# Products on unnormalised chunks ahead of three norms of a two-block fp32 kernel

## What is computed

```python
def modulate(x, g, shift, scale):
    return rms_norm(x, g) * (1 + scale[:, None, :]) + shift[:, None, :]
def swiglu(h, w1, w3, w2):
    return (jax.nn.silu(h @ w1) * (h @ w3)) @ w2
...
        h = modulate(x, norm_g[l, 0], mod[:, 0, 0], mod[:, 0, 1])
        x = x + 0.5 * mod[:, 0, 2][:, None, :] * swiglu(h, ffn1_w1[l], ffn1_w3[l], ffn1_w2[l])
        h = modulate(x, norm_g[l, 1], mod[:, 1, 0], mod[:, 1, 1])
        y = hybrid_mixer(h, w_in[l], fox_f_bias[l], fox_qk_g[l], dsa_qk_g[l], w_br_fox[l], w_br_dsa[l], w_out[l], rope_a, rope_i, top_k)
        x = x + mod[:, 1, 2][:, None, :] * y
        h = modulate(x, norm_g[l, 2], mod[:, 2, 0], mod[:, 2, 1])
        x = x + 0.5 * mod[:, 2, 2][:, None, :] * swiglu(h, ffn2_w1[l], ffn2_w3[l], ffn2_w2[l])
```

## Time and profile before

| | us |
|---|---|
| median of 3 runs | 1995.74 |
| lowest and highest | 1994.92, 1996.67 |
| span of the profiled execution, first to last instruction | 1992.7 |
| TensorE busy (matmuls) | 1961.6 |
| VectorE, ScalarE, GpSimd busy | 901.8, 747.8, 825.9 |
| useful products end and start again around norm 3 | 838.8, 848.3 |
| around norm 4 | 1215.5, 1223.9 |
| around norm 5 | 1616.1, 1624.2 |

### The profile page before, as it was taken

The page is one execution under the profiler, slowest core; times in us unless marked ns, Lnnn a source line. Parts: engine busy times, 40 slices in busy tenths (PEclk is TensorE's granted clock), DMA queues, the critical chain, the costliest instruction groups (busy, mean ns, idle before and its releaser), DMA issues.

```text
span 1992.7 us, 25487 instructions
## 1 busy us (share of the span) xinstructions
PE 1961.6 (98%) x9250; PEld 1552.8 (78%) x9250; DVE 901.8 (45%) x1457; ACT 747.8 (38%) x1241; POOL 825.9 (41%) x361
## 2 busy tenths in 40 slices
PE   7999999999999999999999999999999999999998
PEld 6877656688888888888888888776767878888887
DVE  6772565432632453457662204777872242101111
ACT  5343555432431232333313324436673243222321
POOL 4365321243554345435543443333444434443442
PEclk9999999999999999999999999999999999999999
DMA  6355111243656477548643343332123333333341
GB/s 180 88 142 134 32 44 43 55 102 102 169 155 192 122 186 201 138 118 212 172 105 95 84 116 71 78 75 53 33 54 76 94 75 94 101 100 95 86 115 53
DMA packets 154565, 211.14 MB, mean 106 GB/s; under 512 B 15432, under 2 KB 129640, under 8 KB 154344
## 3 DMA queue, kind: packets, MB, share of 16 engines
q1 hardware_dynamic: 140232, 167.34, 34.0%
q10 hardware_dynamic: 14240, 42.54, 7.1%
HBM read 206.69 MB, written 2.10 MB: 105 GB/s over the span
## 4 chain that ended last, share of the span: by engine, by line
PE 49%; issue 33%; POOL 14%; DVE 2%; DMA 1%; ACT 1%; POOLq 0%; ACTq 0%; SPq 0%; DVEq 0%
PE ps L670 15%; PE ps L672 15%; PE ps L671 15%; POOL wlo L620 13%; PE ps L1164 1%; PE ps L1188 1%; PE ps L769 1%; DMA xrow<-in_x 0%; DVE score L2384 0%; PE ps L787 0%; PE ps L1208 0%; DVE xT L2415 0%; PE ps L950 0%; PE ps L718 0%; DVE st L2006 0%
## 5 line engine op out<-in xcount | busy, mean ns | idle before, releaser
L620 POOL TENSOR_TENSOR wlo<-raw,whi 128x1024 fp32r<-128x1024 f32 (+1 forms) x317 | 779.8, 2475 | 1037.3 <-ACT whi L1458 1015.6
L670 PE MATMUL ps<-hhi,whi 128*128 128x512 f32 x1496 | 592.9, 396 | 7.6 <-POOL wlo L620 3.5
L672 PE MATMUL ps<-hhi,wlo 128*128 128x512 f32 x1496 | 584.2, 390 | 0.0
L671 PE MATMUL ps<-hlo,whi 128*128 128x512 f32 x1496 | 583.7, 390 | 0.0
L1458 ACT ACTIVATE whi<-raw 128x1024 fp32r<-128x1024 f32 x309 | 316.7, 1055 | 385.4 <-PE ps L672 359.6
L670 PEld LDWEIGHTS ps<-hhi,whi 128*128 128x128 f32 x1496 | 281.4, 188 | 75.5 <-issue 12.6
L672 PEld LDWEIGHTS ps<-hhi,wlo 128*128 128x128 f32 x1496 | 281.2, 188 | 59.5
L671 PEld LDWEIGHTS ps<-hlo,whi 128*128 128x128 f32 x1496 | 281.6, 188 | 56.7 <-issue 1.2
L670 PE MATMUL ps<-hidhi,whi 128*128 (+1 forms) x608 | 236.8, 390 | 0.0
L672 PE MATMUL ps<-hidhi,wlo 128*128 (+1 forms) x608 | 236.8, 389 | 0.0
L671 PE MATMUL ps<-hidlo,whi 128*128 (+1 forms) x608 | 236.8, 389 | 0.0
(11 more groups left out here) (401 smaller groups left out, 2353.5 us busy)
## 6 DMA issues: line engine op xcount, KB each, us to landing
raw<-in_ffn_w SPq DMA_DIRECT2D x264, 256.0 KB, 3.8
raw<-in_w_in SPq DMA_DIRECT2D x154, 256.0 KB, 4.0
trig<-in_ada_w ACTq DMA_DIRECT2D x72, 512.0 KB, 4.7
raw<-in_w_up SPq DMA_DIRECT2D x64, 256.0 KB, 4.0
raw<-in_w_down SPq DMA_DIRECT2D x64, 256.0 KB, 3.9
raw<-in_w_out SPq DMA_DIRECT2D x32, 256.0 KB, 3.7
xrow<-in_x ACTq DMA_DIRECT2D x4, 512.0 KB, 6.2
raw<-in_cmp_k_w SPq DMA_DIRECT2D x8, 256.0 KB, 3.7
```

The costliest lines, as they stand in the source:

```text
L620: last = pool.tensor_tensor(lo, src, hi.bitcast(F32), ALU.subtract)
L670: pe.matmul(out_, lhi, rhi, start=first, stop=False)
L671: pe.matmul(out_, lhi, rlo, start=False, stop=False)
L672: return pe.matmul(out_, llo, rhi, start=False, stop=last)
```

## The change

At each of the norms 3, 4 and 5 the first four slabs behind it (96 products) use gain times x, split in XHI (ScalarE) and XLO (VectorE) as soon as a chunk of xT is there, in place of h. The filler is gone. The parts:

- GpSimd makes the five adds of squares (`squares`), between the halves of slabs; VectorE makes XLO in that place. TensorE sums total and last two squares by token (12 matmuls of one column, each two rows of the trace, as before) ahead of the third slab, and spreads half a slab later. ScalarE copies the spread row from PSUM to rstd in SBUF, and VectorE's norm reads it there.
- The banks of these first products are scaled afterwards by VectorE (TENSOR_TENSOR ps, rstd) and the shift's share is added as a bias: sigmoid with bias on ScalarE for the gates, (st + bias) * tmp on VectorE.
- The bias is shift times weights. In the down stage ahead, ScalarE issues four transfers of 512 KB of the first columns of the weights into the place of hhi (`shift_weights`), VectorE adds up 16 weighted pieces of 128x256 (`weight_shifts`), TensorE sums them over the partitions in two pairs (`shift_sums`), and VectorE copies each pair to bias (`biases`).
- In norm 4 the queries (blocks 0 and 1 of fox) are such products.

```diff
@@ pe projection
+                            unscaled = name == "fox" and n < 2
+                            opening = 2 if name == "fox" else 0
...
+                                if unscaled and n == 1:
+                                    square_sums(4) if q == 0 else shift_sums(4, 0)
...
+                                    if unscaled and n == 1 and q == 0 and x == 4:
+                                        norm(4)
...
+                            if unscaled and n == 1:
+                                shift_sums(4, 1)
+                                pe.wait_ge(bias_ready, 2 * STAT[4])
@@ pe ffn_up
+                if h == 0:
+                    blocks(0, True, {2: lambda: square_sums(nn), 3: lambda: shift_sums(nn, 0)})
+                    if f == 0:
+                        turn_modulation(4)
+                    shift_sums(nn, 1)
@@ gpsimd
+            def squares(n):
+                e = STAT[n]
+                for m in range(1, KD - 2):
+                    pool.wait_ge(n_sq, 8 * (e - 1) + m + 1)
+                    if m > 1:
+                        pool.wait_ge(n_add, 5 * (e - 1) + m - 1)
+                    pool.tensor_tensor(SQUARES[m], SQUARES[m - 1], SQUARES[m], ALU.add).then_inc(n_add, 1)
+                if n == 3:
+                    low(AT[FIRST[n]] + 1)
...
-            lows(AT["mixb1"] + SLOTS, AT["mixa2"] + SLOTS)
+            lows(AT["mixb1"] + SLOTS, AT["f1up0"] + 1)
+            squares(3)
+            lows(AT["f1up0"] + 2, AT["fox"] + 2)
+            squares(4)
@@ scalar norm
                         sc.wait_ge(x_ready, X_BEFORE_NORM[n] + m + 1)
+                        sc.activation(XHI[n][m], xT[:, m, :], ACT.Identity, scale=GAIN[n][:, m:m + 1]).then_inc(x_hi, 1)
...
+                    if n != 4:
+                        sc.activation(early[:, n + 2:n + 3], col(C_EPS), ACT.Sigmoid)
+                    high(s0 + SLOTS)
+                    sc.wait_ge(n_all, e + 1)
+                    sc.activation(rstd[:, :], ps[:, 7, :], ACT.Copy).then_inc(rows_ready, 1)
@@ scalar, first_chunks of a ffn_up
+                    high(s0 + 2)
+                    for c in range(2):
+                        sc.wait_ge(ff_m2, u0 + c + 1)
+                        sc.activation(hidhi[:, c, :], tmp[:, 2 + c, :], ACT.Copy).then_inc(ff_hi, 1)
+                    high(s0 + 3)
@@ vector
+            def biases(n, pair):
+                x = 2 * (STAT[n] - 1) + pair + 1
+                ve.wait_ge(ws_sum, x)
+                ve.tensor_copy(bias[:, 2 * pair:2 * pair + 2], ps[:, 6, 8 + 2 * pair:10 + 2 * pair]).then_inc(bias_ready, 1)
...
+            def first_queries(pair):
+                for v in (2 * pair, 2 * pair + 1):
+                    g = G0["fox"] + v
+                    ve.wait_ge(*OUT_DONE[g])
+                    ve.tensor_tensor(tmp[:, v, :], ps[:, g % 4, :], rstd[:, :], ALU.mult).then_inc(scaled, 1)
+                biases(4, pair)
...
-            norm(4)
+            norm(4, {3: lambda: first_queries(0)})
+            first_queries(1)
```

More of the change, by code:

```diff
@@ L146, in mix_kernel @@
         xT = sb("xT", [P, KD, S])
+        HHI = used[0]
         hhi = sb("hhi", [P, KD, S], F32R)
@@ new lines, in gates_scaled, with gates_done @@
+            def gates_scaled(f):
+                n = (3, 5)[f]
+                for c in range(2):
+                    if c == 0:
+                        ve.wait_ge(ff_g, 11 * f + 1)
+                    else:
+                        ve.wait_ge(w_used, AT[f"f{f + 1}up0"] + 2)
+                    ve.tensor_tensor(st[:, c, :], ps[:, c, :], rstd[:, :], ALU.mult).then_inc(scaled, 1)
+                biases(n, 0)
+            def gates_done(f):
+                for c in range(2):
+                    ve.wait_ge(ff_sig, 22 * f + c + 1)
+                    ve.scalar_tensor_tensor(out=tmp[:, c, :], in0=st[:, c, :], scalar=bias[:, c:c + 1], in1=tmp[:, c, :],
+                                            op0=ALU.add, op1=ALU.mult).then_inc(ff_m1, 1)
@@ new lines, in first_chunks @@
+            def first_chunks(f):
+                u0, e = 22 * f, STAT[(3, 5)[f]]
+                for c in range(2):
+                    if c == 0:
+                        ve.wait_ge(ff_u, 11 * f + 1)
+                    else:
+                        ve.wait_ge(w_used, AT[f"f{f + 1}up0"] + 4)
+                    ve.tensor_tensor(st[:, c, :], ps[:, 2 + c, :], rstd[:, :], ALU.mult).then_inc(scaled, 1)
+                biases((3, 5)[f], 1)
+                for c in range(2):
+                    ve.wait_ge(scaled, 4 * (e - 1) + 3 + c)
+                    ve.wait_ge(ff_m1, u0 + c + 1)
+                    ve.scalar_tensor_tensor(out=tmp[:, 2 + c, :], in0=st[:, c, :], scalar=bias[:, 2 + c:3 + c], in1=tmp[:, c, :],
+                                            op0=ALU.add, op1=ALU.mult).then_inc(ff_m2, 1)
+                for c in range(2):
+                    ve.wait_ge(ff_hi, u0 + c + 1)
+                    ve.tensor_tensor(hidlo[:, c, :], tmp[:, 2 + c, :], hidhi[:, c, :].bitcast(F32), ALU.subtract).then_inc(ff_ready, 1)
```

242 lines of the change are left out of this document (173 added, 69 removed).

## The result

The changed kernel takes **2008.34 us** (median of five runs, 2007.81 to 2012.17), the kernel before 1995.74: 12.6 us more, a ratio of 1.0067 with a 95% interval of 1.0054 to 1.0079. The profiled execution of the change is the slowest of the five: it took 2012.17 us, 3.8 above the median, and spans 2010.4. That of the kernel before spans 1992.7; the other runs of that kernel span about 2.2 less than they take, so it was some 0.8 us quicker than its median. The two profiles thus differ by 17.7 us and show about 5 us too much.

What follows compares the result with a forecast made beforehand. TensorE, busy 98% of the span, was taken as the bound, with chains of VectorE holding it after the change. Norm 3 +4.5, norm 4 +6.7, norm 5 -2.5, clock +2.1: +10.8 us, 2006.5 us, range 1996.5 to 2012.

Steps and rivals of the forecast that it cites:

- What bounds and T0: TensorE, busy 98%, bounds the kernel; filler gaps at the three norms are 25.9 us, new products start at T0.
- T0: At each norm, TensorE's slot after the last product of the down stage; later times are counted from it.
- Norm 5, -2.5: TensorE gains 3.5 us if nothing waits, less 1.0 for late h chunks at i = 1: -2.5 us (-1.5 to -3.5).
- Norm 4, +6.7 and 1.3 for the clock: Behind the fourth slab TensorE waits about 10 us for VectorE's last bias copy: +6.7 us; clock dip adds 1.3.
- The lock: VectorE instructions with two SBUF inputs and GpSimd instructions reading SBUF exclude each other: 4.8 us more at norm 3.
- Rival (a): The lock hardly matters and ScalarE's queue adds nothing: +0.1 to +2.7 us, about 1998; chance 0.17.
- Norm 3, +4.5 and 0.8: First ffn stage: modulation chain from unit 48 starts later, TensorE waits some 10 us before i = 2: +4.5, clock 0.8.
- rival (b): The modulation chain behind norm 3 does not bind: -5.4 us, 1990.3; chance 0.11.
- Work costed at nothing: GpSimd's adds, extra weight transfers and weighted sums cost nearly nothing; norm 3's slab 1 up to 1 us late, hidden.
- The clock, 2.1 in all: Two TensorE stands of some 10 us lower the granted clock: 1.3 us at norm 4, 0.8 at norm 3.
- "right" ones: No filler; 10 us wait in norm 4; 8 to 11 before i = 2; clock dips; unit 48 timing; slow scales.
- "wrong" ones: i = 2 below T0 + 52, norm 4's wait under 5 us, or a stand at the second or third slab.

Runs made afterwards that it cites:

- sums_apart: Kernel with norm 5 alone changed, token sums issued in thirds, each ahead of three products, instead of one piece: 1992.45 us, ratio 0.9983.
- bias_early: The change, but in norm 4 VectorE copies the second pair of biases behind h chunk 4's scale, not at the norm's end: 2002.27 us, ratio 1.0032.
- only_norm3: Norm 3 alone as in the change, norms 4 and 5 as in the kernel before: 2002.93 us, ratio 1.0040.
- slab1_early: The change, but in norm 3 ScalarE copies slab 1 ahead of chunk 1 and GpSimd splits it behind its first add: 2016.84 us, ratio 1.0099.
- adds_on_vector: From bias_early, the five adds of squares moved back from GpSimd to VectorE: 2004.46 us, ratio 1.0043.
- units_later: From bias_early, two modulation units moved from block 0 of the first ffn stage into block 1, all later ones with them: 1999.45 us, ratio 1.0018.

## Why the prediction was right, and where a size was off

The forecast was 2006.5 in a range of 1996.5 to 2012; measured 2008.3. In the sum, +10.8 was forecast and +12.6 measured, with an interval from 10.8 to 15.8. Step by step:

**What bounds and T0.** Right. The filler was free room, and the products start in slot T0.

**Norm 5, -2.5.** Right: -2.9 by the medians, -1.9 by the trace. The gap to 3.5 was put down to late h chunks alone; 1.0 us of it was the half clock behind the sums, as sums_apart shows (-2.9 from T0 to the end), and the prediction did not have that.

**Norm 4, +6.7 and 1.3 for the clock.** Right in place: TensorE waits 9.7 us for the bias behind the fourth slab, and bias_early shows the line to be the cause. The size is right too, in part by luck: TensorE goes on at T0 + 37.8 (37.2 predicted), but VectorE's first scale stands at T0 + 19.6 instead of 18.2 (1245.98), because of the half clock behind the sums, and the way from there is 0.9 shorter than reckoned (each bias copy took 0.15 us and not 0.3, for one). Of the +8.8 us from T0 to T0, 7.3 are this wait and 1.5 the clock behind it; 8.0 were forecast. What the prediction missed lies behind that line: without the wait there was still no gain, because of VectorE's chain.

**The lock.** Right: 4.8 us were put on norm 3, and the four places named for them show 0.6, 1.6, 1.1 and 1.5 us in only_norm3. Unit 48 starts at T0 + 45.8 there (46.0 by the +4.5 that was taken; 42.1 by the prediction's sum without the lock). Rival (a), that it hardly matters, falls.

**Norm 3, +4.5 and 0.8.** The mechanism is right, and rival (b) falls: TensorE waited 8.5 to 9.2 us before i = 2 in the traces of that code, and in the five traces with the changed norm 3 that keep the order of the stage i = 2 starts 13.6 to 13.9 us behind unit 48 (14.0 before), in slab1_early too, where both are 9 us later. The size is right in only_norm3, with +4.9 from T0 to T0. Its medians say +7.2, with 5.2 to 10.8 as the interval, so whether the usual execution costs more than the forecast stays open.

**Work costed at nothing.** This is the step that was off, in the slowest execution. The profile of the whole change has +9.3 us from T0 to T0 at norm 3, because TensorE stood for 2.93 us at slab 1, where at most 1 was allowed for, and because the clock fell behind the sums. The prediction put "the extra 2 MB of weights per norm" and "the 16 weighted sums on VectorE" at nearly nothing. In the down stage ahead of norm 3 they are not nothing. The first to show are the transfers. Four of them stand in ScalarE's queue ahead of the transfer of modulation unit 38, which was issued at 762.93 and landed 20.6 us later (the slowest of that stage took 5.4 in the trace before), and VectorE waits for it ahead of the first weighted sum:

```profile
783.58 1.28 DVE L2631 SCALAR_TENSOR_TENSOR Pb<-trig,vec,Pb 128x1024 f32<-128x1024 f32 x1 [15.33 <-DMA trig<-in_ada_w]
...
789.86 0.34 DVE L2150 TENSOR_SCALAR wsum<-early_w,mod 128x256 f32<-128x256 f32 x1
```

and before:

```profile
768.39 1.28 DVE L2436 SCALAR_TENSOR_TENSOR Pb<-trig,vec,Pb 128x1024 f32<-128x1024 f32 x1 [2.49 <-DMA trig<-in_ada_w]
```

In all eight traces with the changed norm 3 one transfer of this stage took 19.1 to 20.6 us and VectorE waited 15.3 to 17.4 us for it; in the six others none took over 8.0, and the longest wait there is 6.4. Unit 38 is 15.2 us late by it. Then come the sums: they took 9.8 us (789.86 to 799.69), as bounded, and stand in VectorE's queue ahead of units 40 to 47. Unit 41 starts at 800.54 instead of 783.84, 16.7 us late, so most of its delay was there before the first sum. VectorE's last unit of the down stage and ScalarE's first row of norm 3 after the change:

```profile
828.04 1.77 DVE L2631 SCALAR_TENSOR_TENSOR PT<-trig,vec,PT 128x1024 f32<-128x1024 f32 x1 [3.31 <-DMA trig<-in_ada_w]
...
830.25 1.28 ACT L1545 ACT_TABLE_LOAD   x1 [3.99 <-DVE PT L2631]
...
845.35 1.04 ACT L1514 ACTIVATE whi<-raw 128x1024 fp32r<-128x1024 f32 x1
...
846.47 2.35 POOL L634 TENSOR_TENSOR wlo<-raw,whi 128x1024 fp32r<-128x1024 f32 x1 [1.65 <-ACT whi L1514]
```

and before:

```profile
816.47 1.28 DVE L2436 SCALAR_TENSOR_TENSOR PT<-trig,vec,PT 128x1024 f32<-128x1024 f32 x1 [3.94 <-DMA trig<-in_ada_w]
...
823.83 1.28 ACT L1489 ACT_TABLE_LOAD   x1
```

The last unit is 11.6 us later, ScalarE enters the norm 6.4 us later and VectorE makes the first chunk of x 5.0 us later (830.46 instead of 825.47). So the copy of slab 1 and GpSimd's half of it come late. In the other seven executions with the changed norm 3 the same delay was nearly used up by then: ScalarE came in between 824.6 and 826.5, where it came in between 823.8 and 825.8 in the six traces with the former norm 3. Slab 1 was in time in five traces of seven (the two others are this one and adds_on_vector; slab1_early is left out). What makes this execution the slow one is not shown; VectorE waited 14.7 us in it for the transfers of units 42 to 47, and 9.4 to 13.6 in the seven others. No run took the transfers or the weighted sums away, so how the two share in the delay, and how much of the spread of the change's runs (4.4 us) is theirs, stays open.

**The clock, 2.1 in all.** Too small for the profiled execution. The two long waits cost 1.5 us behind the bias (the products of line 796 took 2.8 us to the next product, where the earlier trace rows and the row behind it had 1.3) and 2.2 before i = 2 (11 products at 0.43). Behind the sums 1.6 us are lost at each norm. The kernel before lost as much there at norm 3 and 1.4 at norm 4, half of it on fillers, and nothing at norm 5; the prediction took the spread from norm 5, where the clock had not fallen, and had none of this. Some of it is hidden again by the next wait.

**The signs named in the prediction.** Of the "right" ones all but one were in the profile of the change: unit 48 is at T0 + 49.7 there, outside the 43 to 47 that were named, and inside them in only_norm3 (45.8). One of the "wrong" ones was there too, the stand at the second slab. It pointed to the step that was off: the copy was late, and not GpSimd's adds, as GpSimd waited 1.65 us for it.

## To carry to other kernels

Work moved into a gap of TensorE pays only where the next stage was waiting for TensorE: of three like places one gained, because behind the others a chain of VectorE (late adds and modulation units, reciprocals) started later by the new work, and TensorE's lead ended in a wait for it. Before costing such an edit, follow the slowest engine's chain through the whole stage. And ask of every operation or transfer that goes into a queue "where the engine idles" what stands behind it in that queue: here one unit's transfer behind four new ones landed after some 20 us, and in seven executions of eight there was slack enough for it. Of the kernels run, the fastest were norm 5 alone (1992.8 us), the same with the sums apart (1992.5, 0.9983 with 0.9973 to 0.9993), and norms 4 and 5 with the bias and the roots early (1992.6); each is faster than the kernel before and than the change, and they don't differ measurably from each other.

## What the runs showed of the hardware that was not expected

- A piece of 2.6 us of token sums (24 rows of 128x1, fp32) was followed by eight products at 0.43 us instead of 0.227 in 13 of 20 norms, granted clock 0.61 over that stretch; spread out between products, never in 8. At norm 5, with no wait of TensorE ahead of it in the norm, it was 7 of 7 against 0 of 4. The Trainium skill (TensorE: Matmul & The Clock Gate, HAM oscillation — how this bites in real kernels) tells of the clock falling where TensorE waits for transfers; here it fell though the rows show TensorE busy. In the kernel before it fell too, at two norms of three, and its fillers took a part of that on themselves.
- The exclusion of VectorE and GpSimd reaches far from the norms: modulation units (128x1024, both inputs in SBUF) took 1.28 us alone and 3.20 beside GpSimd's halves in units_later, where two halves took 5.65 us instead of 4.7.
- A reciprocal of 128x512 took 3.35 us on VectorE, where a product of that shape took 0.75. Eight of them filled most of a chain of 37.5 us that TensorE had to wait for.
- The transfer of a unit issued behind four new ones of 512 KB on ScalarE's queue landed after 20.6 us (19.1 to 20.6 in the eight traces that have it); in the six traces without these four the slowest of that stage took 5.3 to 8.0.
